# Six key-triangle products of an item multiplied in three pairs of heads instead of one by one

## The chip, the cores and the metric

The program runs on one core of a Trainium2 chip. The metric is the device time of one execution in microseconds (us). The core's engines are PE (TensorE: matmuls, with PEld for its weight loads), DVE (VectorE), ACT (ScalarE), POOL (GpSimd) and SP (SyncE, which issues most DMAs). Each runs its own list of instructions in order and meets the others at semaphores.

## What is computed

Two transformer blocks on 1024 tokens of width 1024 with 256 context tokens. The change touches the preparation of the RWKV branch of the first block: eight heads of 64, two directions. The reference, cut to this:

```python
def rwkv_prepare(u, decay_w0, decay_w2, iclr_a0, iclr_a2, k_k, k_a):
    r, k, v, hw, ha, hg = jnp.split(u, RW_SPLITS, axis=-1)
    kk = heads(k * k_k)
    kk = kk * lax.rsqrt(jnp.maximum(jnp.sum(kk * kk, axis=-1, keepdims=True), 1e-24))
    for d in range(2):
        w_log = -jax.nn.softplus(-(decay_w0[d] + jnp.tanh(hw) @ decay_w2[d])) - 0.5
        a = jax.nn.sigmoid(iclr_a0[d] + ha @ iclr_a2[d])
        decay = jnp.exp(-jnp.exp(heads(w_log)))
        k_d = heads(k * (1 + (a - 1) * k_a))
        dirs.append((decay, kk * heads(a), k_d))
...
    def step(S, inp):
        sa = jnp.einsum('bhvk,bhk->bhv', S, -kk_t)
        S = S * w_t[:, :, None, :] + sa[..., None] * b_t[:, :, None, :] + v_t[..., None] * k_t[:, :, None, :]
```

The kernel runs the scan in chunks of 128 tokens. For that it needs, for each direction, chunk and head, the 128x128 product of the chunk's scaled kk and b keys over the head's 64 features. Only the four 32x32 blocks on the diagonal of each such product ("triangle") are kept here; the solver inverts them.

## The kernel before

**The front.** The function `front` lays four programs side by side on the engines: `Linears` (LIN: the input projections, 128 columns of weights to a tile; one step is 8 times three matmuls of up to 512 columns, L651 to L653, or for the tiles laid out by token 128-column ones, L643 to L645), `Prepare` (PREP: what the reference's rwkv_prepare does, and the triangles), `Window` (the attention, mostly after PREP) and `Solver` (on POOL). A fixed list of steps made at build time sets the order: after LIN step 15 about 1.9 PREP steps follow each LIN step, until PREP has ended with the last of the first 20 tiles. Every engine walks the same list, so the order on PE is fixed and a PREP step that waits holds back all LIN work behind it.

**PREP.** Its work is cut into eight items: four pairs of heads (a pair of heads fills 128 partitions, head e=0 on partitions 0 to 63, e=1 on 64 to 127), each in two halves of five chunks (640 tokens). An item takes 21 steps, called half-steps o=0 to 20, and a new item begins every 8, so that at o=12 to 16 of one item the next stands at o=4 to 8. The tables `ON_DVE`, `ON_ACT` and `ON_PE` name the work of each half-step. On PE: z0, z1 (decay, L1026 with 32 rows), kkc (sum of squares, L1043), a0, a1 (L1026), spread (L1053), bon (L1026 with mats), and the triangles n0 to n5 (L1073). Within one half-step the older item's work comes first.

**The triangles.** An item has 10 of them for each head (two directions by five chunks), 20 in all. `TRIANGLES` cuts them into six groups: n0, n2, n4 are head e=0, units 0 to 3, 4 to 7 and 8 to 9; n1, n3, n5 the same units of head e=1. A group goes into one PSUM bank, 2 for even groups, 3 for odd. Each unit is one fp32 matmul with 64 rows, 128 weight columns and 128 moving columns; the trace has two MATMUL records for each, so a four-unit group is x8 and a two-unit group x4. ACT copies the kept blocks of group m out as d0 to d5 (four ACTIVATEs each, L1007). n2 to n5 wait for the copy of the group two before, which frees the bank; n0 and n1 also wait for DVE's B0, the rest for B1 (all of PREP's DVE work is recorded at L846). `Solver` starts on a batch when SP has stored the copied blocks (L814, L818).

**Who takes what from PE.** DVE waits for kkc, spread and bon, and through ACT's sigmoids (L964) for z0, z1, a0, a1. ACT's copy of a LIN result is L671. The items are n=0 to 7; their n0 start at 194.2, 242.7, 278.1, 324.8, 369.4, 416.2, 485.0 and 530.1 us.

Of the kernel before, what the change touches and what calls it, by code (L numbers as in the profile page):

```python
# [687 lines left out]
class Prepare:  # L688
# [9 lines left out]
    ON_ACT = {3: ["sg0", "sq"], 5: ["sg1"], 6: ["sqrt"], 7: ["a0"], 9: ["a1"],  # L698
              10: ["e10", "e20", "e30", "e11", "e21", "e31"], 13: ["d0"], 14: ["d1"], 15: ["d2", "d3"], 16: ["d4"],
              17: ["d5"]}  # L700
    ON_PE = {2: ["z0"], 4: ["z1"], 5: ["kkc"], 6: ["a0"], 7: ["spread"], 8: ["a1"], 11: ["bon"], 12: ["n0"], 13: ["n1"], 14: ["n2", "n3"], 15: ["n4"],
             16: ["n5"]}
    TRIANGLES = [(m % 2, 4 * (m // 2), (4, 4, 2)[m // 2]) for m in range(6)]

    def __init__(self, C, rw, chunked, v_chunked, bonus, gate_in, blocks, at):
# [246 lines left out]
    def scalar(self, act):  # L952
# [13 lines left out]
        for s in range(self.LEAD, self.slots):  # L966
            for n, o in self.active(s):
# [10 lines left out]
                elif o == 6:  # L978
                    act.wait_ge(self.dstep, dv[n, "rec"])
                    nc.scalar.activation(self.sqk.rearrange("p (t n) -> p t n", n=HD),  # L980
                                         self.rs[n % 2].unsqueeze(2).broadcast_to([P, 10, HD]),
                                         ACT.Sqrt).then_inc(self.astep, 1)
                elif o in (7, 9):
                    d = (o - 7) // 2
                    if n >= 1:
                        act.wait_ge(self.outs[d], 64 * n)
                        act.wait_ge(self.pstep, pv[n - 1, "n5" if d else "n3"])
                    rate(n, d, "a", self.ab[d], "iclr_a0")
                elif o == 10:
                    for d in range(2):  # L990
                        act.wait_ge(self.dstep, dv[n, f"y{d}"])
                        if n >= 1:
                            act.wait_ge(self.outs[d], 64 * n)
                        w, y = self.w[d], self.y[d]
                        for e, src, sign in zip(self.e[d], (w, y if d else w, y), (1, 1 if d else -1, -1)):
                            nc.scalar.activation(e, src, ACT.Exp, scale=sign * KAPPA).then_inc(self.astep, 1)
                elif 13 <= o <= 17:
                    for name in self.ON_ACT[o]:
                        m = int(name[1])
                        e, u0, nu = self.TRIANGLES[m]  # L1000
                        act.wait_ge(self.pstep, pv[n, f"n{m}"])
                        if n >= 1 and m == 0:
                            act.wait_ge(self.diag_out, 16 * n)
                        ps = C.psum[:, 2 + m % 2, 0:nu * CH].rearrange("p (u c) -> p u c", c=CH)
                        for k in range(CH // BK):
                            r = slice(BK * k, BK * (k + 1))
                            a = nc.scalar.activation(self.diag[r, 10 * e + u0:10 * e + u0 + nu, :], ps[r, :, r],  # L1007
                                                     ACT.Copy)
                        a.then_inc(self.astep, 1)
# [6 lines left out]
    def tensor(self, pe):  # L1016
# [12 lines left out]
        for s in range(self.LEAD, self.slots):  # L1029
            for n, o in self.active(s):  # L1030
# [15 lines left out]
                elif o in (6, 8):  # L1046
                    d = (o - 6) // 2
                    pe.wait_ge(self.astep, ac[n, "a0" if d else "sg1"])
                    product(4, self.w2[32:64, d, cols], self.tail[32:64, half])
                elif o == 7:  # L1050
                    pe.wait_ge(self.astep, ac[n, "sqrt"])
                    for t in range(5):
                        mm = pe.matmul(C.psum[:, 6 + t // 4, (t % 4) * P:(t % 4 + 1) * P],  # L1053
                                       self.sqk[:, t * P:(t + 1) * P],
                                       C.mat("ident"), start=True, stop=True)
                    mm.then_inc(self.pstep, 1)
                elif o == 11:
                    pe.wait_ge(self.dstep, dv[n, "bon"])
                    a, m, t = self.lat(n)
                    product(6, C.mat("headsum"), self.out[:, a:a + m])  # L1060
                elif 12 <= o <= 16:
                    for name in self.ON_PE[o]:
                        m = int(name[1])
                        e, u0, nu = self.TRIANGLES[m]
                        if m >= 2:
                            pe.wait_ge(self.astep, ac[n, f"d{m - 2}"])
                        elif n >= 1:
                            pe.wait_ge(self.astep, ac[n - 1, f"d{m + 4}"])
                        pe.wait_ge(self.dstep, dv[n, "B0" if m < 2 else "B1"])
                        for x in range(nu):  # L1070
                            d, c = (u0 + x) // 5, (u0 + x) % 5
                            A, B = (self.results(d)[y][64 * e:64 * e + 64, c * CH:(c + 1) * CH] for y in (0, 2))
                            mm = pe.matmul(C.psum[:, 2 + m % 2, x * CH:(x + 1) * CH], A if d else B, B if d else A,  # L1073
                                           start=True, stop=True)
                        mm.then_inc(self.pstep, 1)
            yield


# [2760 lines left out]
```

## Time and profile before

| | us |
|---|---|
| median of 3 executions | 3521.47 |
| lowest and highest | 3514.03 and 3525.67 |
| the profiled execution | 3513.61 |
| its span in the trace | 3511.8 |
| PE busy in the span | 3248.4 (92%) |
| mean granted clock of TensorE | 0.948 of 2.4 GHz |

The triangles run between 194 and 548 us. All times in the trace count from the first instruction. In the timeline a row is a run of like instructions; the time from its start to the start of the next row is what it takes from PE, and its own length ends with the last result, some 0.07 us into the next row. A bracket at a row's end is the idle time of the engine before it, and what ended it. In the waits view a row sums all waits of one line for another line.

### The profile page before, as it was taken

How to read it: one execution, taken by the hardware profiler on the slowest of the kernel's cores; microseconds unless marked ns; L12 is line 12 of the kernel's file. 1: busy time of each engine (PE TensorE's matmuls, PEld its weight loads, DVE VectorE, ACT ScalarE, POOL GpSimd, SP SyncE). 2: the span in 40 equal slices, each digit the busy share in tenths (PEclk: the TensorE clock that was granted, in tenths of full speed). 3: DMA queues.
4: the chain of work that ended last, by engine and by line, in shares of the span. 5: the costliest groups of instructions: out<-in, count | busy, mean ns of one | idle time of the engine just before them, and what ended most of it. 6: DMA issues, size and time to landing. Idle time of an engine off the chain costs nothing. (4 is left out here: it accounts for less than half of the span.)

```text
span 3511.8 us, 46419 instructions
## 1 busy us (share of the span) xinstructions
PE 3248.4 (92%) x18084; PEld 2592.9 (74%) x18084; DVE 1852.3 (53%) x2662; ACT 1158.3 (33%) x2270; POOL 1555.9 (44%) x1195
## 2 busy tenths in 40 slices
PE   6898999999799999889999999999897999999796
PEld 4766787788598988668888888888775666777465
DVE  4288844546445455586633363336312666565736
ACT  5244431333333333331211021102223665145723
POOL 1215635455143341266666666665451001654432
PEclk9988879999899999999999999999997999999898
DMA  4345435232343342353333333334434221222112
GB/s 179 102 141 150 145 116 181 92 92 70 96 128 106 98 131 63 113 152 93 94 98 99 98 93 99 96 96 114 130 105 124 76 61 43 88 83 60 48 54 78
DMA packets 521310, 358.60 MB, mean 102 GB/s; under 512 B 92561, under 2 KB 477446, under 8 KB 520070
## 3 DMA queue, kind: packets, MB, share of 16 engines
q1 hardware_dynamic: 510438, 325.22, 32.0%
q0 software_dynamic: 4608, 16.78, 1.6%
q10 hardware_dynamic: 6048, 13.63, 1.1%
q8 instruction: 146, 2.39, 0.3%
q14 instruction: 70, 0.57, 0.1%
HBM read 276.85 MB, written 78.18 MB: 101 GB/s over the span
## 5 line engine op out<-in xcount | busy, mean ns | idle before, releaser
L2409 PE MATMUL psum<-place,place 128*128 128x512 f32 x2126 | 856.4, 403 | 63.2 <-POOL place L2387 29.3
L2410 PE MATMUL psum<-place,place 128*128 128x512 f32 x2126 | 837.8, 394 | 0.0
L2411 PE MATMUL psum<-place,place 128*128 128x512 f32 x2126 | 836.9, 394 | 0.0
L2385 POOL CAST place<-place 128x1024 fp32r<-128x1024 f32 (+3 forms) x302 | 298.3, 988 | 1097.0 <-PE psum L2411 650.1
L2387 POOL TENSOR_TENSOR place<-place,place 128x1024 fp32r<-128x1024 f32 (+3 forms) x302 | 692.1, 2292 | 24.2
L2409 PEld LDWEIGHTS psum<-place,place 128*128 128x128 f32 x2126 | 405.8, 191 | 171.5 <-issue 44.8
L2410 PEld LDWEIGHTS psum<-place,place 128*128 128x128 f32 x2126 | 405.9, 191 | 88.7 <-issue 6.6
L2411 PEld LDWEIGHTS psum<-place,place 128*128 128x128 f32 x2126 | 405.2, 191 | 87.0
L651 PE MATMUL psum<-place,place 128*128 128x512 f32 (+1 forms) x712 | 289.3, 406 | 20.9 <-issue 10.2
L652 PE MATMUL psum<-place,place 128*128 128x512 f32 (+1 forms) x712 | 274.5, 386 | 0.0
L653 PE MATMUL psum<-place,place 128*128 128x512 f32 (+1 forms) x712 | 273.9, 385 | 0.0
L607 POOL CAST place<-place 128x1024 fp32r<-128x1024 f32 x44 | 48.9, 1110 | 429.9 <-DMA place<-in_w_in 407.9
L1123 POOL TENSOR_TENSOR solve<-solve 128x31 f32<-128x31 f32 (+15 forms) x310 | 205.9, 664 | 31.2 <-DMA solve<-blocks 8.6
L2500 DVE SCALAR_TENSOR_TENSOR place<-psum,mod,place 128x512 f32<-128x512 f32 x80 | 60.0, 750 | 254.3 <-PE psum L2411 254.3
L651 PEld LDWEIGHTS psum<-place,place 128*128 128x128 f32 x712 | 144.5, 203 | 54.6 <-issue 16.5
L1655 PE MATMUL psum<-place,place 96*128 96x512 f32 (+4 forms) x352 | 142.6, 514 | 26.1 <-DMA place<-gate 15.5
L653 PEld LDWEIGHTS psum<-place,place 128*128 128x128 f32 x712 | 144.1, 202 | 25.5
L652 PEld LDWEIGHTS psum<-place,place 128*128 128x128 f32 x712 | 145.0, 204 | 22.4 <-issue 1.5
L2453 ACT ACTIVATE place<-psum 128x512 f32<-128x512 f32 x64 | 38.1, 596 | 338.1 <-PE psum L2411 338.1
L2524 DVE TENSOR_TENSOR place<-place,place 128x512 fp32r<-128x512 f32 x64 | 116.0, 1812 | 49.6 <-ACT place L2455 49.6
L1708 DVE TENSOR_REDUCE cols<-psum 128x1 f32<-128x256 f32 (+7 forms) x160 | 99.7, 623 | 72.6 <-PE psum L1655 69.3
L671 ACT ACTIVATE place<-psum 128x512 f32<-128x512 f32 (+4 forms) x96 | 51.9, 541 | 232.2 <-PE psum L653 206.1
(331 smaller groups left out, 5510.7 us busy)
## 6 DMA issues: line engine op xcount, KB each, us to landing
place<-in_w_mlp_up SPq DMA_DIRECT2D x64, 512.0 KB, 4.0
place<-in_w_mlp_down SPq DMA_DIRECT2D x64, 512.0 KB, 3.9
place<-in_w_out SPq DMA_DIRECT2D x48, 512.0 KB, 4.1
chunked<-place SPq DMA_DIRECT2D x64, 320.0 KB, 3.6
place<-in_w_in SPq DMA_DIRECT2D x34, 512.0 KB, 5.6
solve<-in_w_ada POOLq DMA_DIRECT2D x32, 512.0 KB, 6.2
place<-in_lru_w_in SPq DMA_DIRECT2D x32, 512.0 KB, 3.9
place<-in_mla_w_in SPq DMA_DIRECT2D x30, 512.0 KB, 4.1
```

The lines of the kernel that those rows point to most:

```text
L651: pe.matmul(ps, self.w_hi[:, j, k, :], hi, start=(k == 0), stop=False)
L652: pe.matmul(ps, self.w_hi[:, j, k, :], lo, start=False, stop=False)
L653: mm = pe.matmul(ps, self.w_lo[:, j, k, :], hi, start=False, stop=(k == end))
L1123: f(*args).then_inc(self.sstep, 1)
L1655: mm = pe.matmul(self.score_at(e)[:, a:a + w], q[:, b * P:(b + 1) * P], k[:, a:a + w], start=True, stop=True)
L1708: nc.vector.reduce_max(mx, ps[:, 0:n], AX_X).then_inc(self.maxed, 1)
L2385: nc.gpsimd.tensor_copy(hi, raw).then_inc(self.w_split, 1)
L2387: nc.gpsimd.tensor_tensor(lo, raw, hi.bitcast(F32), ALU.subtract).then_inc(self.w_split, 1)
L2409: pe.matmul(ps, self.w_hi[:, j, k, :], hi, start=(k == 0), stop=False)
L2410: pe.matmul(ps, self.w_hi[:, j, k, :], lo, start=False, stop=False)
L2411: mm = pe.matmul(ps, self.w_lo[:, j, k, :], hi, start=False, stop=(k == kt - 1))
L2524: tt(t["out_lo"], x, t["out_hi"].bitcast(F32), ALU.subtract).then_inc(self.hid, 1)
```

## The change

The six groups are multiplied in three pairs: n0 with n1, n2 with n3, n4 with n5. Within a pair the loop goes over the units and, inside, over the two heads: unit 0 of head 0 into bank 2, unit 0 of head 1 into bank 3, unit 1 of head 0, and so on. The pairs stand at half-steps 12, 14 and 16. Before, n0 stood at 12, n1 at 13, n2 and n3 at 14, n4 at 15, n5 at 16. A pair waits for the later of the two copies that free its banks (d1 before n2, d3 before n4, the previous item's d5 before n0). On ACT the copies stand where they stood, and each waits for the second group of its pair (`m | 1`).

```diff
@@ -698,8 +698,8 @@
     ON_ACT = {3: ["sg0", "sq"], 5: ["sg1"], 6: ["sqrt"], 7: ["a0"], 9: ["a1"],
               10: ["e10", "e20", "e30", "e11", "e21", "e31"], 13: ["d0"], 14: ["d1"], 15: ["d2", "d3"], 16: ["d4"],
               17: ["d5"]}
-    ON_PE = {2: ["z0"], 4: ["z1"], 5: ["kkc"], 6: ["a0"], 7: ["spread"], 8: ["a1"], 11: ["bon"], 12: ["n0"], 13: ["n1"], 14: ["n2", "n3"], 15: ["n4"],
-             16: ["n5"]}
+    ON_PE = {2: ["z0"], 4: ["z1"], 5: ["kkc"], 6: ["a0"], 7: ["spread"], 8: ["a1"], 11: ["bon"], 12: ["n0", "n1"], 14: ["n2", "n3"],
+             16: ["n4", "n5"]}
     TRIANGLES = [(m % 2, 4 * (m // 2), (4, 4, 2)[m // 2]) for m in range(6)]
 
     def __init__(self, C, rw, chunked, v_chunked, bonus, gate_in, blocks, at):
@@ -998,7 +998,7 @@
                     for name in self.ON_ACT[o]:
                         m = int(name[1])
                         e, u0, nu = self.TRIANGLES[m]
-                        act.wait_ge(self.pstep, pv[n, f"n{m}"])
+                        act.wait_ge(self.pstep, pv[n, f"n{m | 1}"])
                         if n >= 1 and m == 0:
                             act.wait_ge(self.diag_out, 16 * n)
                         ps = C.psum[:, 2 + m % 2, 0:nu * CH].rearrange("p (u c) -> p u c", c=CH)
@@ -1058,21 +1058,23 @@
                     pe.wait_ge(self.dstep, dv[n, "bon"])
                     a, m, t = self.lat(n)
                     product(6, C.mat("headsum"), self.out[:, a:a + m])
-                elif 12 <= o <= 16:
-                    for name in self.ON_PE[o]:
-                        m = int(name[1])
-                        e, u0, nu = self.TRIANGLES[m]
-                        if m >= 2:
-                            pe.wait_ge(self.astep, ac[n, f"d{m - 2}"])
-                        elif n >= 1:
-                            pe.wait_ge(self.astep, ac[n - 1, f"d{m + 4}"])
-                        pe.wait_ge(self.dstep, dv[n, "B0" if m < 2 else "B1"])
-                        for x in range(nu):
-                            d, c = (u0 + x) // 5, (u0 + x) % 5
+                elif o in (12, 14, 16):
+                    first, second = (int(name[1]) for name in self.ON_PE[o])
+                    if first >= 2:
+                        pe.wait_ge(self.astep, ac[n, f"d{second - 2}"])
+                    elif n >= 1:
+                        pe.wait_ge(self.astep, ac[n - 1, f"d{second + 4}"])
+                    pe.wait_ge(self.dstep, dv[n, "B0" if first < 2 else "B1"])
+                    _, u0, nu = self.TRIANGLES[first]
+                    for x in range(nu):
+                        d, c = (u0 + x) // 5, (u0 + x) % 5
+                        for m in (first, second):
+                            e = self.TRIANGLES[m][0]
                             A, B = (self.results(d)[y][64 * e:64 * e + 64, c * CH:(c + 1) * CH] for y in (0, 2))
                             mm = pe.matmul(C.psum[:, 2 + m % 2, x * CH:(x + 1) * CH], A if d else B, B if d else A,
                                            start=True, stop=True)
-                        mm.then_inc(self.pstep, 1)
+                            if x == nu - 1:
+                                mm.then_inc(self.pstep, 1)
             yield
```

On PE, at half-steps 13 and 14 of item 0. place_629, place_623 and place_624, place_630 are the keys of the two directions. L1073 (L1074 after) are the triangles, L1043 is kkc of item 1, L1026 its a0:

```order
 L653 MATMUL psum<-place_52,place_607 128x512
-L1073 MATMUL psum<-place_629,place_623 128x128 x4
 L1043 MATMUL psum<-mats,place_616 128x2 x5
-L1073 MATMUL psum<-place_629,place_623 128x128
-L1073 MATMUL psum<-place_624,place_630 128x128 x3
-L1073 MATMUL psum<-place_629,place_623 128x128
-L1073 MATMUL psum<-place_624,place_630 128x128 x3
+L1074 MATMUL psum<-place_629,place_623 128x128 x2
+L1074 MATMUL psum<-place_624,place_630 128x128 x6
 L1026 MATMUL psum<-place_633,place_635 128x512
```

n1 has left the place ahead of kkc (it now stands with n0, one LIN step earlier), and the eight units of n2 and n3 are interleaved.

Further on, at half-step 15 of item 0, ahead of item 1's spread (L1053), and at half-step 16, ahead of its a1 (L1026):

```order
 L653 MATMUL psum<-place_52,place_607 128x512
-L1073 MATMUL psum<-place_624,place_630 128x128 x2
 L1053 MATMUL psum<-mats,place_616 128x128 x5
 L651 MATMUL psum<-place_52,place_606 128x256
```

```order
 L653 MATMUL psum<-place_52,place_607 128x256
-L1073 MATMUL psum<-place_624,place_630 128x128 x2
+L1074 MATMUL psum<-place_624,place_630 128x128 x4
 L1026 MATMUL psum<-place_633,place_635 128x512
```

n4 has moved from ahead of spread to n5's place ahead of a1, behind one more LIN step. The order of instructions on ACT, DVE, POOL and SP is the same before and after.

## Rows read from the trace of the kernel before

**Rows 1.** The page: span, and each engine's busy time, share and instructions.

```profile
span 3511.8 us, 46419 instructions
PE 3248.4 (92%) x18084; PEld 2592.9 (74%) x18084; DVE 1852.3 (53%) x2662; ACT 1158.3 (33%) x2270; POOL 1555.9 (44%) x1195
```

**Rows 2.** Busy time by stretch; PEclk is the granted share of 2.4 GHz.

```profile
core 0: us, PE busy (x) PEld busy (x) DVE busy (x) ACT busy (x) POOL busy (x), PEclk, DMA share, GB/s
190.00:547.50 357.50, 327.11 (x1518) 261.16 (x1518) 259.66 (x319) 153.51 (x326) 176.81 (x191) 0.81 0.48 143
...
341.00:348.00 7.00, 7.00 (x27) 5.66 (x27) 5.47 (x11) 5.13 (x12) 0.42 (x1) 0.52 0.78 254
...
450.00:494.50 44.50, 44.50 (x176) 39.72 (x176) 18.88 (x23) 11.87 (x19) 13.61 (x16) 0.50 0.39 107
```

**Rows 3.** Waits, 190 to 547.5 us: who for whom, us, times, longest.

```profile
PE psum L1073 <- DVE place L846: 23.1, 7, 8.2
...
DVE cols L846 <- PE psum L1043: 28.3, 4, 17.1
DVE place L846 <- PE psum L1053: 24.2, 6, 7.1
...
DVE place L846 <- ACT place L964: 8.4, 3, 6.9
```

**Rows 4.** Instructions by line, 190 to 570: count, busy us, mean ns, idle before.

```profile
L1073 PE MATMUL psum<-place,place 64*128 64x128 f32 x320 | 48.2, 310 | 23.9 <-DVE place L846 23.1 <-ACT place L1007 0.9
```

**Rows 5.** Timeline of PE, item 0 and others: start, us, line, shapes, count.

```profile
207.00 1.16 PE L1073 MATMUL psum<-place,place 64*128 64x128 f32 x8
208.09 1.28 PE L1043 MATMUL psum<-mats,place 128*128 128x2 f32 x10
209.30 1.71 PE L1073 MATMUL psum<-place,place 64*128 64x128 f32 x16
210.94 2.28 PE L1026 MATMUL psum<-place,place 32*128 32x512 f32 x4
...
221.09 0.71 PE L1073 MATMUL psum<-place,place 64*128 64x128 f32 x4
221.72 1.05 PE L1053 MATMUL psum<-mats,place 128*128 128x128 f32 x7
...
420.59 2.07 PE L1073 MATMUL psum<-place,place 64*128 64x128 f32 x8
```

**Rows 6.** Timeline of PE where two heads' groups meet: item 7, and line L2032.

```profile
547.57 0.72 PE L1073 MATMUL psum<-place,place 64*128 64x128 f32 x8
548.22 0.50 PE L651 MATMUL psum<-place,place 128*128 128x512 f32 x1
...
938.96 0.72 PE L2032 MATMUL psum<-place,place 64*128 64x128 f32 x8
939.60 0.66 PE L2016 MATMUL psum<-mats,place 128*128 128x128 f32 x4
```

**Rows 7.** Timeline, item 1: PE waits for DVE; then DVE waits for PE.

```profile
272.18 0.59 PE L1026 MATMUL psum<-place,mats 128*128 128x384 f32 x1 [1.88 <-DVE place L846]
...
300.51 0.82 DVE L846 TENSOR_TENSOR place<-place,psum 128x640 f32<-128x640 f32 x1 [4.12 <-PE psum L1053]
```

**Rows 8.** Timeline of ACT and DVE behind n4 and n5 of item 4.

```profile
391.73 0.82 DVE L846 TENSOR_TENSOR place<-place,psum 128x640 f32<-128x640 f32 x1 [2.04 <-PE psum L1053]
...
397.86 0.89 ACT L1007 ACTIVATE place<-psum 32x64 f32<-32x64 f32 x4 [4.30 <-PE psum L1073]
...
399.21 0.80 ACT L964 ACTIVATE place<-psum,params 128x640 f32<-128x640 f32 x1 [0.46 <-PE psum L1026]
...
400.04 0.91 DVE L846 TENSOR_SCALAR place<-place,params,omka 128x640 f32<-128x640 f32 x1 [1.25 <-ACT place L964]
```

**Rows 9.** Timeline behind PREP's end: POOL's weight splits, PE's wait for a load.

```profile
556.65 2.40 POOL L609 TENSOR_TENSOR place<-place,place 128x1024 fp32r<-128x1024 f32 x1
...
567.91 1.07 PE L1262 MATMUL psum<-mats,place 128*128 128x128 f32 x8 [3.05 <-DMA place<-in_mem]
```

## The prediction

> **What bounds the kernel now.** The page first: PE is busy for 3248.4 of 3511.8 us [rows 1], so time taken from PE counts unless somebody else holds the end of that stretch. The triangles all lie between 194 and 548 us, so I read that stretch alone: by line, the 320 records of L1073 take 48.2 us of PE [rows 4]. Then the waits there, in both directions [rows 3]: PE waits for DVE ahead of a triangle seven times, 23.1 us (always n0, but for one 0.37 us before n2), and DVE waits for PE ten times ahead of kkc's and spread's consumers (28.3 and 24.2 us) and three times for the sigmoid of a1 (8.4 us). So the stretch is a ring: PE goes n0, z1, n1, kkc, n2, n3, a0, n4, spread; DVE takes spread and works some 25 us on its own up to B0; PE waits for B0 at the next n0. A microsecond taken from PE between n0 and spread is kept if DVE had to wait at spread (it then starts earlier, and so does the next n0), and lost if DVE did not wait.
>
> **What a pair costs.** A group of four units takes PE from 207.00 to 208.09, 1.09 us; a group of two from 221.09 to 221.72, 0.63 us; n2 followed at once by n3 from 209.30 to 210.94, 1.64 us [rows 5], less than two groups alone (2.18), so where the groups of two heads touch they already overlap in part. How far a full interleave overlaps is shown twice [rows 6]. In item 7, n4 and n5 stand back to back with both banks free: eight records, two units of each head, take 547.57 to 548.22, 0.65 us, as much as one such group alone. And L2032 has the shape and the very order of the change (64 rows, 128 columns, the two heads innermost, a bank for each): eight records from 938.96 to 939.60, 0.64 us. I take it that the second head costs 0.01 us. A pair of four units is then 1.10 us, one of two 0.65.
>
> Per item: n0 and n1, 2.18 to 1.10, saves 1.08. n2 and n3, 1.64 to 1.10, saves 0.54. n4 and n5, 0.63 + 0.65 to 0.65, saves 0.63. Together 2.25 us at full clock, all of it ahead of the next item's spread, since n4 is moved behind it. The bounds: at the low end nothing is saved and the overlap that n2 with n3 has now is lost (0.54 more per item); at the high end the second head is free. The value stands at the high end, because L2032 is the same instruction in the same order.
>
> The Trainium skill (TensorEngine Tiling (Array Packing), Overview) gives row tiling of matmuls with at most 64 rows up to a factor of two, which taken on all 48.2 us would be 24 us instead of the 18 of eight items by the rows; the same page (Restrictions and Gotchas) says that different row tiles can't write one PSUM bank at the same time, and the change does give them a bank each. The trace agrees with the factor in [rows 6], and shows in the 1.64 us of [rows 5] why less is left to win.
>
> **What moves beside it.** (a) n1 a half-step earlier needs B0 and the previous d5, both there before n0 starts. (b) n2 now waits for d1 as n3 did; d0 and d1 are copied during the LIN step that lies between, so no wait, and item 7's wait of 0.64 us before n3 goes. (c) n4 later needs d3, which is done some 5 us before. (d) ACT waits longer for d4, until n5: two copies of 0.9 us [rows 8] now stand between the pair and the sigmoid of a1, where one stood and ended 0.46 us before a1's product was there (399.21). So that sigmoid comes about 0.45 us later relative to PE. Behind it wait DVE's keys. DVE stood waiting there in item 4 (1.25 us, 400.04), after item 0 (0.2 us) and after item 5 (6.93 us, the longest of [rows 3]). (e) LIN's copy L671 may also stand behind d4, by up to 1.5 us; LIN alternates two banks, so PE doesn't see it, and SP's next weight load is that much later, while PE never waits for a weight split in this stretch.
>
> **The sum, item by item.**
> - Item 0: DVE waits at kkc and 7.1 us at spread (the longest of its kind, [rows 3]). Kept 2.25, less 0.6 for (d): 1.65.
> - Item 1: DVE doesn't wait for PE from 224 until 300.51, and PE waits for DVE at 272.18 and at the next n0 [rows 7]. Everything is lost: 0.
> - Item 2: DVE waited 4.12 us at spread (300.51, [rows 7]), more than 2.25. Kept 2.25.
> - Item 3: waits of about 3.5 us at kkc and at spread. Kept 2.25.
> - Item 4: DVE waited 2.04 us at spread (391.73, [rows 8]), but the sigmoid of a0 comes 0.25 us behind, and that of a1 has (d). Kept 1.8.
> - Item 5: PE is at half clock (1.2 GHz): n1 at 420.59 takes 2.0 us instead of 1.09 [rows 5]. PE then runs without a wait until 530, and DVE waits for it (6.93 us at a1). Kept 2.0 + 0.54 + 0.63 = 3.2. If the clock comes back at the same moment as before, LIN work moves into the slow time and only about 2.1 is kept.
> - Item 6: PE without waits, DVE waits up to 17.1 us [rows 3]. Kept 2.25.
> - Item 7: n4 and n5 overlap already. n1 with n2 (1.64), a wait of 0.64 (in the 0.9 of [rows 4]) and n3 (1.09) make 3.4 us and become 1.10: 2.3.
>
> Sum: 1.65 + 0 + 2.25 + 2.25 + 1.8 + 3.2 + 2.25 + 2.3 = 15.7 us.
>
> Does it reach the end? At 559 PE takes up a tile whose split POOL ends at 559.05 [rows 9]; POOL had been busy without a break since 520.6, so item 7's 2.3 us are first lost there. But PE then idles 3.05 us at 567.91 for a load that SP issues after an evacuation of PE's [rows 9]; that load comes earlier, and the 2.3 are had back. From there to the end of the window attention (919 us) PE waits for nothing that doesn't itself follow PE, and the next stage begins behind a barrier. So 15.7 us go through. From the profiled execution's 3513.6 that is 3497.9; it lies 7.9 under the median of the runs, and from the median it is **3505.8, say 3506 us**.
>
> **The clock** is the cost that the trace can't price. The granted clock falls to half for stretches of 7 us and more after the PREP work is bunched: 341 to 348 at 0.52 directly behind item 3's n1, kkc, n2, n3, and likewise after the same bunch of items 0 and 6 [rows 2]; and from 450 to 494.5 it stays at 0.50 though PE is never idle. A bunch that is 1.6 us shorter, in which both heads' rows work at once, could spare such a fall, or shift one.
>
> **Rivals.**
> - A, the ring swallows more: DVE, ahead of schedule by 2 us per item, stops waiting at spread (through ACT's delayed sigmoids or B1), and PE waits longer at n0. The 23.1 us of [rows 3] speak for it, DVE's 52.5 us of waits against. Then only the part from item 5 on, where PE has no wait, is kept, 7.8 us: 3513.7, say 3514.
> - B, clock gained: the three falls of 7 us behind the bunches of items 0, 3 and 6 go; at half clock each cost 3.5 us. 15.7 + 10.5 = 26.2: 3495.
> - C, slower: the clock falls where the change thins out PE's steps (kkc and spread now stand without a triangle beside them) and stays low, as it does from 450 to 494.5 [rows 2]. Place: 348 to 416 us, where PE is busy 60 us at a mean 0.90. At half clock that work takes 108 us, 48 more, of which PE's idle 8 cover a part: +40 against -15.7: 3546. It decides as soon as more than 26 us of now fast PE work runs slow. Against it: the bunches, not their absence, come ahead of the falls. The Trainium skill (TensorE: Matmul & The Clock Gate, Part 1) has the clock follow how busy the engine has been; 450 to 494.5 with PE busy 44.50 of 44.50 us at 0.50 shows that busy in the trace is not enough.
> - D, the pairs don't overlap (the change doesn't do what it says): then n2 with n3 loses its 0.54 in eight items and item 7's n4 with n5 its 0.63: +5: 3526. [rows 6] speak against it.
>
> **How the numbers follow.** Forecast 0.66, A 0.12, B 0.14, C 0.04, D 0.04. About 0.3%, 10.6 us, is what a measurement of this kernel can tell from no change, so faster means below 3510.9. The three executions before lie 11.7 us apart, mostly the clock, so the forecast spreads over some 3498 to 3514, 0.08 of its 0.66 above 3510.9. Faster: 0.58 + 0.14 = 0.72. The same: 0.08 + 0.12 + 0.04 = 0.24. Slower: 0.04. The range from 3492 to 3518 holds the forecast, A and most of B, with C, D and the tails outside, under 0.2.
>
> **What would show it.** In the profile after: L1074 busy about 27 to 30 us instead of 48.2; a four-unit pair x16 in 1.1 us; DVE's waits for L1053 shorter by about 1 us or more each, and PE's wait for B0 at n0 about as long as before, but 2 us longer at item 2; ACT's second copy directly behind its first at d4 and d5; PREP's last triangles at about 532 instead of 548 us, and the window attention's end about 15.7 us earlier. Wrong would be: records of the two heads one after another (D); n0's waits summing to over 30 us (A); or a PEclk over 190 to 548 us that differs from 0.81 [rows 2] by more than 0.03 (B, C).

## The result, and the profile after

| us | before | after |
|---|---|---|
| median, lowest to highest (4 executions each) | 3521.56, 3514.03 to 3525.67 | 3480.61, 3478.20 to 3486.19 |
| the profiled execution, its span | 3513.61, 3511.8 | 3480.35, 3478.6 |
| mean granted clock of it | 0.948 | 0.956 |

The ratio is 0.989, 95% interval 0.987 to 0.991: some 41 us faster, where 15.7 were forecast. The kernel is faster, as said, but by more than the range (3492 to 3518) allowed. The stretch with the triangles, by the busy times; its end is the last triangles of item 7, at 547.5 before [rows 2] and now at 506.9:

```profile
core 0: us, PE busy (x) PEld busy (x) DVE busy (x) ACT busy (x) POOL busy (x), PEclk, DMA share, GB/s
190.00:506.90 316.90, 277.32 (x1526) 220.87 (x1526) 269.13 (x320) 153.26 (x326) 180.45 (x186) 0.89 0.55 162
```

Set against [rows 2], the stretch is 357.5 - 316.9 = 40.6 us shorter. PE's busy time in it falls by 327.11 - 277.32 = 49.8 us, and its idle time grows from 30.4 to 39.6 us. Which lines got shorter, by line on PE, 190 to 510 us (count, busy us, mean ns, idle before):

```profile
L1074 PE MATMUL psum<-place,place 64*128 64x128 f32 x320 | 27.1, 310 | 30.3 <-DVE place L846 30.3
L643 PE MATMUL psum<-place,place 128*128 128x128 f32 x80 | 22.3, 279 | 0.0
```

The triangles fall from 48.2 [rows 4] to 27.1, so 21.1 of the 49.8 is theirs. The mean of one record is still 310 ns: no record got shorter, but the records of the two heads now lie side by side. The other 28.7 us come from instructions that the change doesn't touch. L643 is a case: it belongs to the one tile of this stretch that is laid out by token (the value columns, 240 matmuls of 128 columns), which took 366 ns each before:

```profile
L643 PE MATMUL psum<-place,place 128*128 128x128 f32 x80 | 29.3, 366 | 0.0
```

Same instructions, fewer nanoseconds: that is the clock, and PEclk says so, 0.89 instead of 0.81. The change's own part is as forecast. The timeline of PE after (start, us, line, shapes, count):

```profile
210.33 1.16 PE L1074 MATMUL psum<-place,place 64*128 64x128 f32 x16
211.42 1.12 PE L1026 MATMUL psum<-place,place 32*128 32x512 f32 x2
...
223.94 0.71 PE L1074 MATMUL psum<-place,place 64*128 64x128 f32 x8
224.59 1.34 PE L1026 MATMUL psum<-place,place 32*128 32x512 f32 x4
```

A pair of four units takes 1.09 us (210.33 to 211.42; 1.10 was forecast) and a pair of two 0.65. The waits, 190 to 506.9 us (who for whom, us, times, longest):

```profile
PE psum L1074 <- DVE place L846: 30.3, 7, 9.7
DVE cols L846 <- PE psum L1043: 12.8, 4, 4.6
PE psum L1026 <- DVE place L846: 9.6, 5, 3.4
DVE place L846 <- PE psum L1053: 7.7, 3, 4.1
DVE place L846 <- ACT place L964: 2.5, 3, 1.6
```

DVE waits 23.0 us for PE and for the sigmoid. Before, these three sums made 60.9 [rows 3], and one more wait, of 11.5 us for L1026 at 474.93, made it 72.4. Not all of that relief is the pairs': the two longest waits of before (11.53 and 17.10 us) ended at 475 and 500 us and lay wholly or for the most part in the stretch at half clock from 450 to 494.5. PE waits 30.3 us for DVE ahead of n0, where it was 23.1.

**Where the clock came from.** Before, PE was granted half clock from 450 to 494.5 us, without being idle [rows 2]. That stretch is most of the token tile. How the fall looked before, and the same place of the program after (n5 or the pair n4 with n5 of item 5, a1 of item 6, and the tile going on):

```profile
448.24 0.71 PE L1073 MATMUL psum<-place,place 64*128 64x128 f32 x4
448.88 1.34 PE L1026 MATMUL psum<-place,place 32*128 32x512 f32 x4
450.15 0.47 PE L643 MATMUL psum<-place,place 128*128 128x128 f32 x1
450.42 0.41 PE L644 MATMUL psum<-place,place 128*128 128x128 f32 x1
```

```profile
435.87 0.71 PE L1074 MATMUL psum<-place,place 64*128 64x128 f32 x8
436.51 1.34 PE L1026 MATMUL psum<-place,place 32*128 32x512 f32 x4
...
437.78 0.33 PE L643 MATMUL psum<-place,place 128*128 128x128 f32 x1
437.94 0.28 PE L644 MATMUL psum<-place,place 128*128 128x128 f32 x1
```

Before, a 128-column record of the tile is 0.28 us long up to the triangles and 0.41 behind them. After, it stays at 0.28. One line's records over the whole tile (durations of one, shortest, median and longest, in ns; first and last start in us), first of before and then of after:

```profile
L643 PE MATMUL psum<-place,place x80: 273/415/882, 437.4 to 484.2; 128*128 128x128 f32 x80
```

```profile
L643 PE MATMUL psum<-place,place x80: 272/275/516, 425.0 to 455.6; 128*128 128x128 f32 x80
```

The tile with the PREP work among it takes 46.8 us before and 30.6 after, 16.2 us less. And the windows of after show no fall there:

```profile
424.00:458.00 34.00, 34.00 (x286) 31.70 (x287) 31.79 (x39) 15.94 (x32) 21.84 (x25) 1.00 0.49 142
```

**What was given back.** From the end of the stretch to the end of the span it is 2964.3 us before and 2971.7 after, so 7.4 of the 40.6 are lost again, and 33.2 are left, the difference of the spans. One part is that PE meets POOL's weight splits ahead of their time. PE's waits of L651 for them behind the stretch, first of before and then of after, and the longest that is new in the kernel after:

```profile
PE psum L651 <- POOL place L609: 6.1, 2, 3.5
```

```profile
PE psum L651 <- POOL place L609: 9.9, 4, 4.3
```

```profile
522.14 0.50 PE L651 MATMUL psum<-place,place 128*128 128x512 f32 x1 [3.61 <-POOL place L609]
```

The longest of after, 4.3 us at 657.39, stood before too, with 3.52 at 695.07. The 3.05 us for which the kernel before waited for a load at 567.91 [rows 9] are gone. Set against each other matmul by matmul, the kernel after is some 41 us ahead up to 558 us of before, 38 from there to 900, and 36 or less from the window attention's end on; the small losses behind it no run took apart.

### The profile page after: what moved, and what is told of

Read it like the earlier page. It is cut to its first block and busy times, and to the rows that moved or that the text cites. A ratio compares the mean times of both kernels' runs of the same rounds, so it can differ in the third digit from the quotient of the medians.

```text
span 3478.6 us, 46396 instructions
## 1 busy us (share of the span) xinstructions
PE 3200.1 (92%) x18084; PEld 2552.5 (73%) x18084; DVE 1854.3 (53%) x2662; ACT 1159.4 (33%) x2270; POOL 1565.8 (45%) x1195
## 5 line engine op out<-in xcount | busy, mean ns | idle before, releaser
L651 PE MATMUL psum<-place,place 128*128 128x512 f32 (+1 forms) x712 | 285.7, 401 | 26.6 <-issue 11.1
L653 PE MATMUL psum<-place,place 128*128 128x512 f32 (+1 forms) x712 | 271.0, 381 | 0.0
L652 PE MATMUL psum<-place,place 128*128 128x512 f32 (+1 forms) x712 | 270.9, 380 | 0.0
L651 PEld LDWEIGHTS psum<-place,place 128*128 128x128 f32 x712 | 141.9, 199 | 60.9 <-issue 16.8
```

What stands on the lines that cost most here:

```text
L651: pe.matmul(ps, self.w_hi[:, j, k, :], hi, start=(k == 0), stop=False)
L652: pe.matmul(ps, self.w_hi[:, j, k, :], lo, start=False, stop=False)
L653: mm = pe.matmul(ps, self.w_lo[:, j, k, :], hi, start=False, stop=(k == end))
```

## The experiments

All sets are compared by their own runs of the kernel before, on the same chip. Two theories went in. T: the token tile sits on an edge, where the granted clock either holds at 2.4 GHz to its end or falls to 1.2 GHz and stays there for some 44 us, and one small step of the change tips it; that is one event of about 20 us. D: the gain is spread, each shorter bunch of PREP work sparing a little clock, with no single place that matters. (These letters are not those of the prediction's rivals.) Four runs on one chip first (e1 to e4); the kernel before had a median of 3518.96 there, over 22 executions.

**e1, the kernel before once more**, unchanged, to see whether the fall is of that one execution.

> The kernel before, unchanged, for a second trace. The change gave 41 us where 15.7 were expected. In the trace before, TensorE runs at half clock (1.2 GHz) from 450 to 494.5 us, which begins right behind n5 and a1 of the items around 448 us, inside the value tile that is laid out by token (128-column matmuls, L643 to L645); in the trace after this stretch is absent. Theory T (trap): the fall at 450 happens in every execution of the kernel before, and once fallen the clock stays low until the 128-column tile is over. Then this trace shows it again, within a few us of 450 to 494. Rival S (scatter): the fall depends on the execution; then this trace need not have it, and its time may be 20 us lower.

3517.93 us, one execution. The windows of its trace:

```profile
454.50:498.50 44.00, 44.00 (x174) 39.26 (x173) 19.10 (x23) 11.75 (x19) 13.64 (x16) 0.50 0.40 110
```

The same 44 us at 0.50 with PE busy throughout. The waits ahead of n0 are 27.9 us here and 23.1 in [rows 3], so that sum moves by 5 us between two executions of one kernel.

**e2, the moves without the interleave.** The groups stand where the change puts them, but one head's units come after the other's.

```diff
-                    for x in range(nu):
-                        d, c = (u0 + x) // 5, (u0 + x) % 5
-                        for m in (first, second):
-                            e = self.TRIANGLES[m][0]
+                    for m in (first, second):
+                        e = self.TRIANGLES[m][0]
+                        for x in range(nu):
+                            d, c = (u0 + x) // 5, (u0 + x) % 5
```

> The change without the interleave: the pairs stand at half-steps 12, 14 and 16 as in the kernel after, but within a pair all units of head 0 come before those of head 1. By the trace of before, heads back to back overlap partly: n0 with n1 1.64 us instead of 1.10, n2 with n3 1.64, n4 with n5 0.65 as interleaved. Theory I (the interleave carries the gain beyond the moves): 0.54 us more twice in each of eight items, some 8 us slower than the kernel after where PE bounds, ratio to before about 0.991, and if the clock depends on both heads' rows working at once at n4 and n5, it is not disturbed, since there the two groups overlap anyway. Rival: the clock falls at the value tile again, then 20 us more and ratio about 0.997.

3488.98 us (3487.8 to 3492.79, 7 executions), ratio 0.994 [0.991, 0.997]. Lines on PE, and one pair of four in the timeline:

```profile
L1074 PE MATMUL psum<-place,place 64*128 64x128 f32 x320 | 38.0, 315 | 24.6 <-DVE place L846 24.6
```

```profile
210.44 1.71 PE L1074 MATMUL psum<-place,place 64*128 64x128 f32 x16
212.07 1.12 PE L1026 MATMUL psum<-place,place 32*128 32x512 f32 x2
```

To put the groups side by side takes the triangles from 48.2 to 38.0 us, and the interleave from 38.0 to 27.1. A pair of four one after the other is 1.63 us (the 1.64 of [rows 5]), interleaved 1.09. This kernel has no long fall either (PEclk 1.00 from 424 to 470 us). Against after's 3480.61, measured on another chip, the interleave is worth some 8.4 us (against 3474.96, after's median in a later set, some 14). The ratio given is not that of the two medians, 0.9915, which lies in its interval; the interval is 21 us wide, so the size of this step is rough.

**e3, one place alone.** The kernel before, but for item 5, where n4 is moved behind n5's place and interleaved with it. By rows that is worth 0.6 us.

```diff
+    PAIRED = 5
...
+                    if eng == "pe" and n == self.PAIRED:
+                        names = {15: [], 16: ["n4", "n5"]}.get(o, names)
...
-                        act.wait_ge(self.pstep, pv[n, f"n{m}"])
+                        act.wait_ge(self.pstep, pv[n, "n5" if n == self.PAIRED and m == 4 else f"n{m}"])
...
+                            for g in ((4, 5) if n == self.PAIRED and m == 5 else (m,)):
+                                e = self.TRIANGLES[g][0]
```

> The kernel before with one place changed: in item 5 alone n4 and n5 are multiplied unit by unit at half-step 16 (all other items and groups as before). It takes 0.6 us from PE. Theory T (trap at the value tile): the window around n5 and a1 at 448 us has more rows at work, the clock doesn't fall there, and the stretch from 450 to 494 runs at full clock: 0.6 + about 20 us, ratio about 0.994. Rival D (the surplus is spread over many small clock falls and bunches): under 2 us, ratio 0.9995.

3501.85 us (3493.06 to 3505.95, 10 executions), ratio 0.9953 [0.993, 0.998]: 17 us from one place of 0.6 us. The windows, where e1 had 0.50:

```profile
454.50:485.50 31.00, 31.00 (x224) 27.39 (x223) 20.88 (x27) 15.94 (x30) 14.67 (x17) 1.00 0.66 195
```

T holds and D as the whole story falls. The ten executions lie in two groups, four at 3493 to 3496 and six at 3501 to 3506; both lie below the 18 slower ones of the kernel before (3513 and up). What parts the two is open, since only one execution, of the upper group, was profiled.

**e4, the change without its last pair.** n4 back at half-step 15 and n5 alone at 16, all else as after.

```diff
-             16: ["n4", "n5"]}
+             15: ["n4"], 16: ["n5"]}
...
-                        act.wait_ge(self.pstep, pv[n, f"n{m | 1}"])
+                        act.wait_ge(self.pstep, pv[n, f"n{m if m > 3 else m | 1}"])
...
```

> The change without its last pair: n0 with n1 and n2 with n3 as in the kernel after, n4 at half-step 15 and n5 at 16, apart, as before. By the sum 0.63 us less is won in about six items, 4 us. Theory T: n5 stands alone beside a1 inside the value tile again, the clock falls there and stays low: 4 + 20 us slower than the kernel after, ratio to before about 0.995, with a stretch of about 40 us at half clock. Rival D: 4 us slower than the kernel after, ratio about 0.990.

3500.24 us (3481.48 to 3509.95, 10 executions), ratio 0.994 [0.9915, 0.9964]. The profiled execution (3500.63) has the fall back:

```profile
437.20:481.50 44.30, 44.30 (x184) 39.51 (x183) 20.99 (x26) 14.12 (x24) 15.00 (x18) 0.50 0.38 104
```

The executions fall in two groups: three at 3481 to 3485 and seven at 3497 to 3510. So the kernel stands on the edge and lands on either side of it; I take the three for executions without the fall, which is argued, since only one was profiled.

**Second set (e5 to e8): what does the edge look at?** The kernel before had a median of 3521.66 there, over 13 executions.

**e5, more work in the same place.** The kernel before with one fp32 matmul of constants (128 rows, 512 columns, two records) added between n5 of item 5 and a1 of item 6; nobody reads its result.

```diff
+                    if n == 6 and o == 8:
+                        pe.wait_ge(self.astep, ac[5, "d4"])
+                        pe.matmul(C.psum[:, 2, :], C.mat("ident"), C.mats[:, 0:512], start=True, stop=True)
```

> The kernel before plus work: one fp32 matmul over all 128 rows and 512 columns (constants, result never read) between n5 of item 5 and a1 of item 6, where the clock falls at 448 to 450 us. It costs 0.9 us of PE. So far the kernel before came out in two groups, 18 executions at 3513 to 3528 us and 4 at 3493 to 3499. Theory T (the fall comes because n5 and a1, with 64 and 32 rows, leave the array thinly used there, and the 128-column tile then keeps the clock low): with full rows at work the fall is gone, all executions near 3496, ratio about 0.994. Rival M (it was moving or pairing the triangles, or PE's finishing earlier, that kept the clock): 0.9 us slower, the two groups as before, ratio 1.000.

3501.68 us (3493.96 to 3521.69, 10 executions, nine of them at or below 3511.29), ratio 0.9956 [0.994, 0.998]. A kernel with 1 us more to do is 20 us faster, so rival M of the expectation falls. The timeline at the place, and the windows:

```profile
453.59 0.71 PE L1076 MATMUL psum<-place,place 64*128 64x128 f32 x4
454.23 1.13 PE L1050 MATMUL psum<-mats 128*128 128x512 f32 x2
455.28 1.34 PE L1026 MATMUL psum<-place,place 32*128 32x512 f32 x4
```

```profile
454.50:486.00 31.50, 31.50 (x219) 27.03 (x220) 19.56 (x26) 14.49 (x28) 14.35 (x18) 1.00 0.61 173
```

**e6 and e7, the token tile one tile earlier**, in the kernel before and in the changed one: other PREP work then lies among it. The edit is the same in both.

```diff
-        tiles += [column(C_K, both, padded(kraw, 0)),
-                  column(C_V, [(a, n, a) for a, n in chunks(ALL)], token_rows, by_token=True)]
+        tiles += [column(C_V, [(a, n, a) for a, n in chunks(ALL)], token_rows, by_token=True),
+                  column(C_K, both, padded(kraw, 0))]
```

> The kernel before with the value tile (128-column matmuls) one tile earlier, ahead of the key tile of the window. It then lies from about 399 us, beside item 5's bon and n0, where PE waits for DVE and the clock falls in every trace (405, 416 us). Theory T: the clock can't come back inside the tile, so every execution has a low stretch of 40 us or more from 405 or 416: no group of fast executions, 3513 to 3535 us, ratio 0.997 to 1.006. Rival (the place of the tile doesn't matter): times and groups as before, ratio 1.000 with one execution in five at 3495.

> The kernel after with the same swap of the two tiles. Theory T: now the changed kernel is caught too, by the waits at item 5's bon and n0 (397 and 409 us in its trace), and the change is worth only what it takes from PE: 14 to 18 us less than the swapped kernel before, so 3498 to 3515 us, and 20 to 30 us slower than the kernel after. Rival: it stays at 3480, ratio 0.989.

e6: 3502.06 us (3496.22 to 3503.18, 4 executions), ratio 0.994 [0.992, 0.995]; e7: 3480.47 (3475.54 to 3488.83, 4), ratio 0.988 [0.986, 0.989]. Both forecasts missed. They had reckoned with PE's waits at item 5's bon and n0 and a fall with them; in e6's trace PE has no idle time there (27.50 of 27.50 us), and the tile ran its first 27.5 us at full clock and fell only then:

```profile
404.00:431.50 27.50, 27.50 (x221) 25.43 (x220) 25.17 (x25) 11.61 (x19) 24.13 (x23) 1.00 0.51 139
431.50:455.50 24.00, 24.00 (x106) 22.16 (x106) 11.65 (x18) 8.57 (x22) 8.54 (x10) 0.50 0.32 95
```

So with the tile elsewhere the slow stretch is 24 us long instead of 44, in the one execution that was profiled. Between these two kernels the change is worth 3502.06 - 3480.47 = 21.6 us, nearer to the 15.7 of the sum than the 41 of the real pair is. The profiled execution of e7 is the slowest of its four (3488.83), and it has a fall of its own that begins inside the tile (PEclk 0.92 from 391 to 428 us), so the 21.6 hold some clock too.

**e8, the pairs half a step later.** The changed kernel with its pairs at half-steps 13, 15, 17 and the copies at 14, 16, 18, because PE's largest wait was the one for B0 ahead of n0.

```diff
-              10: ["e10", "e20", "e30", "e11", "e21", "e31"], 13: ["d0"], 14: ["d1"], 15: ["d2", "d3"], 16: ["d4"],
-              17: ["d5"]}
-    ON_PE = {2: ["z0"], 4: ["z1"], 5: ["kkc"], 6: ["a0"], 7: ["spread"], 8: ["a1"], 11: ["bon"], 12: ["n0", "n1"], 14: ["n2", "n3"],
-             16: ["n4", "n5"]}
+              10: ["e10", "e20", "e30", "e11", "e21", "e31"], 14: ["d0", "d1"], 16: ["d2", "d3"],
+              18: ["d4", "d5"]}
+    ON_PE = {2: ["z0"], 4: ["z1"], 5: ["kkc"], 6: ["a0"], 7: ["spread"], 8: ["a1"], 11: ["bon"], 13: ["n0", "n1"], 15: ["n2", "n3"],
+             17: ["n4", "n5"]}
...
```

> The kernel after with its pairs one half-step later: n0 with n1 at 13, n2 with n3 at 15, n4 with n5 at 17, the copies at 14, 16 and 18. In the trace after PE waits 29 us before n0 for DVE's B0, and each time the clock falls with it. Theory W (PE comes too early): a half-step later kkc or a LIN step fills these waits, DVE gets z1 and kkc sooner, and the falls at 192, 312 and 360 us shrink: 10 to 20 us faster than the kernel after, ratio about 0.984. Rival R (DVE is the holder of the ring there, so PE only waits elsewhere): within 5 us of the kernel after, ratio 0.988 to 0.990.

3463.01 us (3462.07 to 3471.06, 4 executions), ratio 0.984 [0.982, 0.985], faster than both kernels. Its windows, and its waits, 190 to 501.1 us:

```profile
190.00:501.10 311.10, 281.33 (x1553) 221.46 (x1552) 272.88 (x321) 153.28 (x327) 187.64 (x195) 0.92 0.57 169
```

```profile
PE psum L1026 <- DVE place L846: 14.9, 5, 6.5
...
PE psum L1026 <- ACT place L964: 5.5, 6, 1.3
PE psum L1074 <- DVE place L846: 4.8, 5, 1.3
```

The wait ahead of the triangles falls from 30.3 to 4.8 us; waits of L1026 grow by 5.3 (for DVE) and 5.5 (for ACT's sigmoids), and PE's idle time in the stretch is 29.8 instead of 39.6 us. PEclk is 0.92 instead of 0.89, so part of the gain is clock again; how it splits no run shows.

**Third set (e9 to e11).** The kernel before had a median of 3519.66, over 7 executions. **e9, a thin filler:** e5's matmul with 32 rows instead of 128, to see whether it is the share of the array's rows that the clock follows.

```diff
...
+                        pe.matmul(C.psum[:, 2, :], C.mat("ident", 32), C.mats[0:32, 0:512], start=True, stop=True)
```

> As the kernel with the filler, but the filler uses 32 rows of the array instead of 128: the same 512 columns in fp32, the same 0.9 us of PE, the same place behind n5 of item 5. The full-row filler made 9 of 10 executions fall into the lower group (3494 to 3511 us). Theory T as it stands (what counts at that place is how much of the array works, not how long PE is busy): the thin filler doesn't help, most executions keep the 44 us stretch at half clock and take 3515 to 3528 us, ratio 1.000. Rival P (it is the time or the shift of 0.9 us that matters, or merely that PE is busy): as the full-row filler, near 3501, ratio 0.9955.

3502.61 us (3502.06 to 3511.12, 4 executions), ratio 0.9956 [0.994, 0.997], as much as with 128 rows; all four lie below the seven of the kernel before (3513.67 and up). The timeline shows that the thin matmul runs beside a1, which stands on other rows (454.97 and 454.98), and the windows show the clock:

```profile
454.33 0.71 PE L1076 MATMUL psum<-place,place 64*128 64x128 f32 x4
454.97 0.69 PE L1050 MATMUL psum<-mats 32*128 32x512 f32 x1
454.98 0.69 PE L1026 MATMUL psum<-place,place 32*128 32x512 f32 x1
...
456.25 0.33 PE L643 MATMUL psum<-place,place 128*128 128x128 f32 x1
```

```profile
454.50:486.00 31.50, 31.50 (x211) 27.19 (x212) 18.90 (x23) 13.43 (x26) 15.69 (x18) 0.95 0.62 177
```

The tile itself (443.5 to 474.1 us) stays at full clock to its end; the 0.95 comes from short falls behind it. A filler with a quarter of the rows holds the clock up just as well, so the number of rows that it fills doesn't decide. And it took nothing from PE: n5, filler and a1 take 1.92 us together (454.33 to 456.25), where n5 and a1 took 1.91 before (448.24 to 450.15). So the time that rival P forecast came out, but of its reasons the 0.9 us and the shift are ruled out: what follows stands where it stood.

**e10 and e11, after and the later pairs once more**, unchanged, on one chip.

> The kernel after, unchanged, beside the next on the same chip and for a second trace. Theory T: no stretch at half clock in the value tile, time within 3476 to 3490 us, one group. If now and then the tile is caught, single executions stand near 3500.

> The kernel with the pairs at half-steps 13, 15 and 17, which took 3463.0 us, unchanged, for a comparison with the kernel after on the same chip: 15 to 20 us below it again, 3460 to 3472 us, ratio to the kernel before 0.984.

e10: 3474.96 us (3473.27 to 3477.69, 4 executions), ratio 0.987 [0.986, 0.989]; e11: 3464.14 (3463.35 to 3467.88, 4), ratio 0.984 [0.983, 0.986]. The change is worth 45 us in this set, and the half step 10.8 more: less than the 15 to 20 that the forecast of e11 had. The second trace of after has no fall in its tile either (PEclk 1.00 from 424 to 460 us).

**e12, the same delay without the work.** The kernel before, where PE waits for the copy d5 at the filler's place and multiplies nothing more. W: it is the work that holds the clock. Q: any shift of the tile by a microsecond does. The kernel before had a median of 3521.03 in this set, over 13 executions.

```diff
+                    if n == 6 and o == 8:
+                        pe.wait_ge(self.astep, ac[5, "d5"])
```

> The kernel before, but at the place of the two fillers (behind n5 of item 5) PE computes nothing and waits some 0.9 us for ACT's copy d5. Both fillers, with 128 rows and with 32, kept the clock up at the value tile (medians 3501.7 and 3502.6 us), so the rows used are not what decides. Left are: W, work in whatever number of rows (more matmul columns at that place) keeps it up; then idle time doesn't, and most executions stay at 3515 to 3528 us with the 44 us stretch at half clock, ratio 1.000. Q, a shift of what follows by 0.9 us is enough; then also here the lower group, near 3502, ratio 0.995.

3522.28 us (3516.72 to 3528.77, 10 executions), ratio 1.001 [0.999, 1.003]. PE stands still for 0.99 us ahead of a1, and the fall comes at that place again, at 447.7 us:

```profile
448.09 2.50 PE L1026 MATMUL psum<-place,place 32*128 32x512 f32 x4 [0.99 <-ACT place L1007]
```

```profile
447.80:495.40 47.60, 47.31 (x179) 41.26 (x180) 19.48 (x24) 12.11 (x21) 13.34 (x17) 0.50 0.38 105
```

A microsecond of work is worth 20 us, a microsecond of idling nothing. W holds. By itself e12 would leave open that the idle time undid what the shift gave; e9 meets that, where work came in without any shift.

**The steps in one table.** Medians of the first set where they have one:

| kernel | us | step |
|---|---|---|
| before | 3518.96 | |
| e3, item 5's last pair alone | 3501.85 | -17.1, the long fall (triangles 0.6) |
| e2, all moves, no interleave | 3488.98 | -12.9 |
| after (its own set) | 3480.61 | -8.4, the interleave |
| e8, half a step later (second set) | 3463.01 | -17.6; -10.8 on one chip (e10, e11) |

The rows of after and e8 come from other chips, and e2's interval is wide, so how the 21 us behind the long fall split over the moves and the interleave is known only roughly.

## Why the prediction was wrong

The direction and the mechanism of the pairs were right; the size was not, and the step that failed is the term behind the sum, **the clock**, which was called "the cost that the trace can't price" and put at nothing.

- **What a pair costs: right.** 1.09 and 0.65 us against 1.10 and 0.65, and 27.1 us for all against the 27 to 30 that it named. The triangles gave 21.1 us where its items add up to 19.0 before the ring; part of the rest is clock.
- **The ring: right in kind.** DVE's waits for L1053 fell from 24.2 to 7.7 us. The ring took 3.3 us in the forecast; PE's idle time grew by 9.2 in the profiled pair. Part of that isn't the change's. The first n0 stands ahead of every moved instruction and already waits 2 us longer than the 5.6 of before, as it does in e1, where nothing was changed (7.7):

```profile
197.27 1.01 PE L1074 MATMUL psum<-place,place 64*128 64x128 f32 x6 [7.63 <-DVE place L846]
...
363.41 0.98 PE L1074 MATMUL psum<-place,place 64*128 64x128 f32 x5 [6.60 <-DVE place L846]
```

  e1 has 27.9 us of waits ahead of the triangles and e10 has 29.2, against 23.1 and 30.3: so the repeats put the growth of that sum at 1 to 7 us. The mark "over 30 us would be A" was just met (30.3) and was drawn too near to the spread of one kernel. A as a loss of half the gain did not happen. What holds in both repeats is item 4: 3.8 and 4.7 us of wait before, 6.6 and 6.6 after, so there the 1.8 us that the sum kept were mostly lost.
- **(d), ACT's second copy: no loss in the sum.** DVE waited 8.4 us for the sigmoids before [rows 3] and waits 2.5 now; 6.93 of the 8.4 was the one wait behind item 5 (it ended at 451.16). The second copy was not tried by itself.
- **Does it reach the end: only in part.** It said that all would go through; of 40.6 us 7.4 were given back, part of it at new waits for POOL's splits such as the 3.61 us at 522.14. The step looked at [rows 9] for 2.3 us. The wait of 3.05 us for a load that it meant to win back is gone, as it said. With 41 us to pass, PE is early enough to meet POOL again.
- **The clock: priced 0, was 28.7 us.** That is PE's busy time outside the triangles, for the same instructions. About 16 of it is the token tile (46.8 to 30.6 us from its first to its last start), and e3 shows 17 us of the median behind the pair of item 5 alone. The stretch stood in [rows 2], at 0.50 and with PE busy, and the text used it twice: as an example of a fall, and as the pattern for rival C, a loss. That the same 44.5 us could go was no rival. At half clock they cost 22 us, and that was the price to put on a case of its own. The prediction did name the sign: a PEclk off 0.81 by more than 0.03 would be B or C, and it came out at 0.89.
- **Rival B: right in sign and in its three places, and too small.** It had 3495 and the three falls of 7 us behind the bunches of items 0, 3 and 6. In the traces of before and e1 all three are there (0.51 or 0.52 over 7 us each). In after the one behind item 0 is down to 3.4 us, and the bunches of items 3 (333 to 341 us) and 6 (465 to 475 us) have none behind them:

```profile
329.00:359.00 30.00, 26.53 (x146) 20.55 (x144) 26.75 (x35) 15.96 (x32) 21.51 (x26) 1.00 0.48 138
458.00:492.00 34.00, 31.35 (x171) 25.07 (x169) 26.18 (x30) 18.13 (x39) 21.27 (x23) 1.00 0.63 183
```

  In e10 all three are gone. Behind items 0 and 3 all seven traces with the old bunches (before, e1, e3, e5, e6, e9, e12) have a fall of 6.8 to 10.2 us, and the four with the new pairs at half-steps 12 and 14 (after, e4, e7, e10) one of 3.4 us or none. The granted clock of the traces, added up, gives what half clock cost: 66.7 us from 190 to 547.5 before and 35.9 from 190 to 506.9 after, 30.8 less. The long fall is 22.2 of that and B's three places are 8.5, near B's 10.5; the other small falls, lengthened and shortened, even out. What B lacked is the long one. No run took the three away one by one; that the shorter bunches did it rests on these traces.
- **Rivals C and D: no.** No stretch of fast work turned slow, and x16 in 1.09 us rules out D.
- **The range.** It took the distance between single executions of before (11.7 us) for the clock's whole play. Over all sets, the kernel before was timed 59 times beside e1: 53 executions lie between 3513 and 3530 us, and six between 3493 and 3499. None of the six was profiled; e3 and e5, which have no long fall, have medians of 3502, so I take 3496 to 3502 for the kernel before without it. From there to after's 3481 it is 15 to 21 us. That the low end meets the 15.7 of the sum is luck in part: these us hold the 8.5 of the three small falls, which the sum had at nothing, and they are what is left after losses behind PREP, which it also had at nothing. The three executions shown all lay in the upper group.

## What to carry to other kernels

Look in the windows for a stretch where PE is busy without a break at PEclk 0.50, and price it as a case of its own, in both directions: half its length can come back (22 us by the clock; e3's median fell by 17) through an edit worth 0.6 us. When a kernel's executions fall in two groups, find out which group the trace shows before the sum is set against the median, and profile one of the other group too, which was not done here. And when a bunch of work gets shorter, place it again: here the same pairs half a step later, where their operands are ready, gave 10.8 us more.

## What the runs showed of the chip

- TensorE was granted 1.2 GHz for 44 us while it was busy without a gap (44.00 of 44.00 us in e1), most of the time on the tile of 128-column matmuls. The same matmuls held 1.00 to the tile's end in after, e10 and e3, where the clock had not fallen inside it: either level can last there. The Trainium skill (TensorE: Matmul & The Clock Gate, Part 1) says that "the default state is throttled, and activity releases the throttle"; by the busy time of the trace that would have ended the slow stretch early, and it did not. Where page and trace differ, the trace decides.
- Work, not time, tips it: an extra matmul that took 1.05 us of PE made the kernel 20 us faster (3501.68 against 3521.66); one with 32 rows, beside a1 and taking no time of its own, made it 17 us faster (3502.61 against 3519.66); and 0.99 us of extra idling changed nothing (3522.28 against 3521.03).
- Which property of the work counts stays open; e9 only speaks against the rows that it fills. Nor is it settled why the kernel before, by its times, misses the fall in about one execution of ten, or why e4 does in three of ten.
